# A third set of input buffers for the recurrence, and every third low half of the mixer's weights made by GpSimd

## The reference

```python
def first_block(x, c, norm_g, w_ada, b_ada, w_in, ...):
    mod = silu(c) @ w_ada + b_ada                 # shift, scale, gate
    h = rms(x, norm_g) * (1 + scale) + shift
    proj = h @ w_in                               # 2048 -> 8 * 1024 columns
    a_q, a_k, a_v, a_z, g_q, g_f, g_i, g_z = split(proj)
    att = chunk_attention(a_q, a_k, a_v) * silu(a_z)      # 8 heads of 128
    hg = hgrn2(g_q, g_f, g_i) * silu(g_z)                 # 8 heads of 128
    return x + gate * (concat(att, hg) @ w_out)

def hgrn2(q_raw, f_raw, i, lb, o_g):
    q = silu(q_raw)
    logf = log(lb + (1 - lb) * sigmoid(f_raw))
    k = (1 - lb) * sigmoid(-f_raw)
    # in chunks of 64 rows, with state S and b = cumsum(logf) in the chunk:
    #   o = (q * exp(b)) @ S + sum over s <= t of (q_t . exp(b_t - b_s) . k_s) v_s
    #   S = exp(b_last) * S + (k * exp(b_last - b))^T @ v
    return rms(o, o_g)
```

## Time and profile before

| | before |
|---|---|
| median of 3 runs, us | 1598.51 |
| lowest and highest run, us | 1595.97, 1599.43 |
| span of the profiled execution, us | 1599.0 (the page gives no other time of it) |
| TensorE busy, us | 1573.0 (98%) |
| VectorE busy, us | 1154.1 (72%) |
| ScalarE busy, us | 862.4 (54%) |
| GpSimd busy, us | 151.6 (9%) |
| TensorE's granted clock, mean | 0.994 |

### The profile page before, as it was taken

One profiled execution on the slowest core, in us unless ns is written; L12 is line 12 of the kernel. 1 busy time (PEld: TensorE's weight loads), 2 busy tenths in 40 slices (PEclk: granted clock), 3 DMA queues, 4 the chain that ended last, 5 costly groups with the idle time before them and its releaser, 6 DMA issues.

```text
span 1599.0 us, 24289 instructions
## 1 busy us (share of the span) xinstructions
PE 1573.0 (98%) x9650; PEld 1400.7 (88%) x9650; DVE 1154.1 (72%) x1696; ACT 862.4 (54%) x1321; POOL 151.6 (9%) x164
## 2 busy tenths in 40 slices
PE   8998999989999999999999999999999999999999
PEld 6787889988999999988799888888888888888887
DVE  6797867877778886759778777777777777455544
ACT  6855546767665555655556454544444444444442
POOL 0000000321221220034213000000000000000000
PEclk9999999999999999999999999999999999999999
DMA  9999975533457774343244545555455454555552
GB/s 373 369 343 349 365 285 209 188 114 121 180 189 267 285 272 179 132 158 132 97 144 178 189 170 199 184 186 210 172 197 191 179 211 175 205 199 185 198 196 105
DMA packets 47825, 331.02 MB, mean 207 GB/s; under 512 B 5281, under 2 KB 6689, under 8 KB 8417
## 3 DMA queue, kind: packets, MB, share of 16 engines
q1 hardware_dynamic: 45184, 312.20, 53.5%
q0 software_dynamic: 2240, 17.04, 2.8%
q10 hardware_dynamic: 290, 0.25, 0.1%
HBM read 327.37 MB, written 2.10 MB: 206 GB/s over the span
## 4 chain that ended last, share of the span: by engine, by line
PE 89%; DVE 5%; DMA 3%; ACT 2%; issue 1%; POOL 0%; SPq 0%; ACTq 0%; DVEq 0%; POOLq 0%
PE ps L1173 20%; PE ps L1174 11%; PE ps L1169 9%; PE ps L1170 8%; PE ps L1171 8%; PE ps L1228 5%; PE ps L1227 5%; PE ps L1226 5%; PE ps L1216 4%; PE ps L1217 3%; PE ps L1218 3%; DVE wl L1916 2%; DMA raw<-in_wts 1%; DMA xs<-in_xN 1%; PE ps L1384 1%; PE ps L1351 1%
## 5 line engine op out<-in xcount | busy, mean ns | idle before, releaser
L1916 DVE TENSOR_TENSOR wl<-raw,wh 128x1024 fp32r<-128x1024 f32 x512 | 626.2, 1236 | 282.4 <-ACT wh L1519 281.9
L1519 ACT ACTIVATE wh<-raw 128x1024 fp32r<-128x1024 f32 x512 | 531.3, 1054 | 377.2 <-PE ps L1228 130.6
L1173 PE MATMUL ps<-hA,wh 128*128 128x512 f32 x1408 | 488.7, 390 | 0.0
L1174 PE MATMUL ps<-hA,wl 128*128 128x256 f32 x1408 | 397.0, 282 | 0.0
L1173 PEld LDWEIGHTS ps<-hA,wh 128*128 128x128 f32 x1408 | 264.2, 188 | 55.3
L1174 PEld LDWEIGHTS ps<-hA,wl 128*128 128x128 f32 x1408 | 266.1, 189 | 0.0
L1169 PE MATMUL ps<-hA,wh 128*128 128x256 f32 x752 | 219.5, 292 | 0.0
L1170 PE MATMUL ps<-hA,wh 128*128 128x256 f32 x752 | 211.7, 282 | 0.0
L1171 PE MATMUL ps<-hA,wl 128*128 128x256 f32 x752 | 211.7, 282 | 0.0
L1169 PE MATMUL ps<-hB,wh 128*128 128x256 f32 x576 | 164.4, 285 | 0.8 <-DVE work L2362 0.4
L1170 PE MATMUL ps<-hB,wh 128*128 128x256 f32 x576 | 161.1, 280 | 0.0
(11 more groups left out here) (303 smaller groups left out, 2077.9 us busy)
## 6 DMA issues: line engine op xcount, KB each, us to landing
raw<-in_wts SPq DMA_DIRECT2D x256, 1024.0 KB, 4.8
raw<-in_ada SPq DMA_DIRECT2D x36, 1024.0 KB, 6.1
side<-in_ada POOLq DMA_DIRECT2D x12, 1024.0 KB, 8.5
work<-in_memN SPq DMA_DIRECT2D x2, 1024.0 KB, 8.9
xs<-in_xN POOLq DMA_DIRECT2D x1, 2048.0 KB, 20.6
xs<-in_xT POOLq DMA_DIRECT2D x2, 1024.0 KB, 7.8
out_rows<-xs SPq DMA_DIRECT2D x8, 256.0 KB, 2.4
wp<-in_dt SPq DMA_DIRECT2D x8, 128.0 KB, 2.7
```

The lines of the kernel that those rows point to most:

```text
L1173: e.matmul(ps[bank][:, :], w1, hl, start=first, stop=False)
L1174: i = e.matmul(ps[bank][:, T:2 * T], w2, hl[:, 0:T], start=False, stop=last)
L1519: e.activation(wh[:, h % WS, :], raw[:, n % RAW, part * HALF:(part + 1) * HALF], ACT.Copy).then_inc(s_hi)
L1916: e.tensor_tensor(wl[:, h % WS, :], src, wh[:, h % WS, :].bitcast(F32), ALU.subtract).then_inc(s_lo)
```

## The change

- `fin`, `qin` and `zin` become lists of four: pair 0 and pair 3 share one slot, pair 1 has the other, and pair 2 has a new buffer `third` of three tiles of 128 x 512 (`INPUT_SET = (1, 0, 2, 1)`). It lies in memory that is free in this part of the program.
- The evacuation of pair 2's inputs waits for no other pair, that of pair 3's for pair 0's last step. In the order only the tiles of pair 3 call `until`, for `("rt", 0)`. Since `kks` and `Es` still have two slots, the task `rf` of pairs 2 and 3 now waits by itself for `rt` of the pair two before (`rec_head`).
- While `share` is on, from the mixer's first tile to the end of the first six tiles of `w_out`, every half whose number divides by `POOL_SHARE = 3` has its low half made by GpSimd: halves 84, 87, ... 156, 25 of them. They count on a semaphore of their own, `wlo_pool`. All who waited for a low half (TensorE, and SyncE's queue for a free slot of `raw`) now wait for the counter of the engine that makes it, by `low_done`. The planner books them on GpSimd's clock with 2.6 us instead of on VectorE's with 1.24.

All other steps are the same, in another order: `HOLD` and the costs are unchanged, but the planned clocks run differently. Both orders are equal up to half 84 or so and again from the end of `w_out` on.

```diff
@@
+INPUT_SET = (1, 0, 2, 1)
...
-BLOCK, HI, LO, TTR = 0.35, 1.05, 1.24, 2.4
+BLOCK, HI, LO, POOL_LO, TTR = 0.35, 1.05, 1.24, 2.6, 2.4
+POOL_SHARE = 3
...
                 at = self.run("act", HI, self.pe_at.get(self.split - WS, 0.0))
-                self.low_at[self.split] = self.run("dve", LO, at + HOP) + HOP
+                if self.share and self.split % POOL_SHARE == 0:
+                    self.pool_low.add(self.split)
+                    self.low_at[self.split] = self.run("pool", POOL_LO, at + HOP) + HOP
+                else:
+                    self.low_at[self.split] = self.run("dve", LO, at + HOP) + HOP
...
+    def rec_head(p):
+        while p >= 2 and ("rt", p - 2) not in o.done:
+            yield
+        yield from stages(("rf", p), REC_HEAD)
...
+    o.share = True
     for kind, n in MIX:
-        if kind != "az" and n >= 2:
-            o.until(("rt", n - 2))
+        if kind != "az" and n == 3:
+            o.until(("rt", 0))
...
         if kind == "f":
-            o.add(5, ("rf", n), stages(("rf", n), REC_HEAD))
+            o.add(5, ("rf", n), rec_head(n))
...
         o.s_half(line[i:i + 8], "C")
+    o.share = False
...
+        third = nc.alloc_sbuf_tensor_at("third", [P, 3, 512], F32, offset=hB_off + 32 + 12 * 2048)
...
+        fin, zin, qin = ([(pair[:, 0, :], pair[:, 1, :], third[:, i, :])[n] for n in INPUT_SET] for i, pair in enumerate((fin2, zin2, qin2)))
...
+        def low_done(h):
+            by_pool = sum(n <= h for n in o.pool_low)
+            return (s_plo, by_pool) if h in o.pool_low else (s_lo, h + 1 - by_pool)
...
                 if j == 0:
-                    e.wait_ge(s_lo, h + 1)
+                    e.wait_ge(*low_done(h))
...
                 if k == "sigmoid":
                     e.wait_ge(*after(("f", 2 * pr + 1), "act", "ev"))
+                    if pr >= 2:
+                        e.wait_ge(*after(("rt", pr - 2), "dve", "lo"))
...
                     pr = j // 2
-                    if pr >= 2:
-                        e.wait_ge(*after(("rt", pr - 2), "dve", "lo"))
+                    if pr == 3:
+                        e.wait_ge(*after(("rt", 0), "dve", "lo"))
...
                 if b[0] == "low":
-                    split(*b[1:])
+                    if b[1] not in o.pool_low:
+                        split(*b[1:])
...
+            def split(h, n, part):
+                src = raw[:, n % RAW, part * HALF:(part + 1) * HALF]
+                e.wait_ge(s_hi, h + 1)
+                e.tensor_tensor(wl[:, h % WS, :], src, wh[:, h % WS, :].bitcast(F32), ALU.subtract).then_inc(s_plo)
```

More of the change, by code:

```diff
@@ L253, in __init__ @@
         self.second = set()
+        self.share = False
+        self.pool_low = set()
         self.events = []
@@ L913, in program @@
         s_side = [sem(f"side{i}") for i in range(4)]
-        s_hi, s_lo, s_half, s_mid = (sem(n) for n in ("whi", "wlo", "half", "mid"))
+        s_hi, s_lo, s_plo, s_half, s_mid = (sem(n) for n in ("whi", "wlo", "wlo_pool", "half", "mid"))
         chains = {f"{c}_{e}": sem(f"{c}_{e}") for c in ("ev", "pre", "lane0", "lane1", "lane2", "lane3", "lane4", "lane5")
@@ L965, in program @@
         a1 = 0
-        fin, a1 = carve(a1, 2, 512, of=early)
-        qin, a1 = carve(a1, 2, 512, of=early)
-        zin, a1 = carve(a1, 2, 512, of=early)
+        fin2, a1 = carve(a1, 2, 512, of=early)
+        qin2, a1 = carve(a1, 2, 512, of=early)
+        zin2, a1 = carve(a1, 2, 512, of=early)
+        fin, zin, qin = ([(pair[:, 0, :], pair[:, 1, :], third[:, i, :])[n] for n in INPUT_SET] for i, pair in enumerate((fin2, zin2, qin2)))
         kk, a1 = carve(a1, 512, of=early)
@@ L1121, in load @@
                     else:
-                        e.wait_ge(s_lo, 2 * o.widx[b] + 2)
+                        e.wait_ge(*low_done(2 * o.widx[b]))
+                        e.wait_ge(*low_done(2 * o.widx[b] + 1))
                 src = ada[o.at[n]] if o.entries[n][0] == "a" else wts[o.at[n]]
@@ L1374, in rec_end @@
                     e.wait_ge(*after(t, "act", "sq"))
-                    e.matmul(ps[6][:, :], ones[:], fin[:, t[1] % 2, :], start=True, stop=True).then_inc(mark(t, "pe", "ss"))
+                    e.matmul(ps[6][:, :], ones[:], fin[t[1]], start=True, stop=True).then_inc(mark(t, "pe", "ss"))
             def softmax(t, k, bank, pairs, causal, v, B):
@@ L2091, in rec_end @@
                 pr = t[1]
-                f, r, z = (x[:, pr % 2, :] for x in (fin, qin, zin))
+                f, r, z = (x[pr] for x in (fin, qin, zin))
                 if k == "r1":
@@ L2408, in rec @@
                 pr = t[1]
-                f = fin[:, pr % 2, :]
+                f = fin[pr]
                 def decay(n):
@@ L2498, in ev @@
                     e.wait_ge(*after(t, "pool", "d"))
+            def split(h, n, part):
+                src = raw[:, n % RAW, part * HALF:(part + 1) * HALF]
+                e.wait_ge(s_hi, h + 1)
+                e.tensor_tensor(wl[:, h % WS, :], src, wh[:, h % WS, :].bitcast(F32), ALU.subtract).then_inc(s_plo)
             e.wait_ge(raw_in[2], 16)
             for b in o.beats:
-                if b[0] == "sload":
+                if b[0] == "low":
+                    if b[1] in o.pool_low:
+                        split(*b[1:])
+                elif b[0] == "sload":
                     i = b[1]
```

26 lines of the change are left out of this document (13 added, 13 removed).

## The result

The changed kernel took 1611.69 us (median of 4 runs, 1610.03 to 1615.05), the kernel before 1598.97 (4 runs). The ratio is 1.0088, with a 95% interval of 1.0066 to 1.0111: 12.7 us slower by the medians, 14 by the ratio. The forecast was 1588.5 us with a range up to 1597.0, and 0.07 on slower.

What follows compares the result with a forecast made beforehand. The prediction took the kernel to be bound by TensorE's matmuls, busy 1573.0 of 1599.0 us. It summed 1599.0 - 13.7 + 3.7 + 0 = 1589.0 us, 1588.5 against the median, with a range of 1583.0 to 1597.0.

Steps and rivals of the forecast that it cites:

- The third buffer's gain: Forced waits ahead of pairs 2 and 3 go: 8.5 us idle, 4.2 clock, 1.0 unpacked matmuls, 13.7 us won.
- small matmuls that aren't packed: In the forced stretches, small matmuls' waits below the trace's grain count as busy; 1 us of gain, 0 to 4.
- What is late next: Moved steps crowd ahead of the output projection and at pair 0's and 1's ends: 3.7 us lost, 1 to 8.
- six forced rows: Ahead of the output projection at half 144, TensorE has six rows without a projection block: 1.9 us lost.
- the two old stretches: Forced places behind halves 103 and 111, without projection matmuls: 12.7 us lost on 40 rows, 0.32 us a row.
- Rival 1: Stalls move to pair 3's end at half 152: some 4 us there, 2 scattered, 1594.5 us; chance 0.17.
- GpSimd's low halves: 25 subtractions moved from VectorE to GpSimd, estimated at 1.9 us each; 0 us on the path setting the end.
- the bound of 1.6: At each GpSimd low half, VectorE would lose 1.6 us when its next instruction reads two SBUF inputs.
- my net of -5 us: VectorE's net work from the 25 moved low halves, taken as -5 us, between -31 and +9.
- TensorE never idle at 36 of 40 us: In window 520 to 560 VectorE was busy 35.75 of 40 us, TensorE never idle: VectorE near nine tenths costs nothing.
- Rival 3: VectorE falls behind through port blocking at halves 92 to 108 and 140 to 144: 3 us, 1591.5; chance 0.15.
- rival 2: GpSimd's low halves come late behind decay steps, 1 us TensorE stall at each of 15: 1603.5 us; chance 0.08.

Runs made afterwards that it cites:

- e3_same_order_dve: The changed kernel's order to the row, but VectorE makes the 25 low halves instead of GpSimd: 1603.68 us, ratio 1.0034 to the kernel before.
- e13_no_hold_rec2: As e12_no_hold_rt3, also without the hold table's entries for pair 2's recurrence: 1587.82 us, ratio 0.9933 to the kernel before.
- e6_gates_later: As e3_same_order_dve, with the output gate's sums in the w_out stretch two tiles later: 1594.69 us, ratio 0.9969 to the kernel before.
- e9: The kernel before with only the output gate's sums two tiles later: 1599.81 us, ratio 1.0011 to the kernel before.
- e7_both: As e6_gates_later, with forced waits for attention 4 to 7 and the gates two halves into w_out: 1596.83 us, ratio 0.998.
- e12_no_hold_rt3: As e6_gates_later, without the hold table's two entries for pair 3's end: 1593.66 us, ratio 0.9967 to the kernel before.
- e8: The kernel before's order to the row, two input buffers, but GpSimd makes the 25 low halves: 1603.32 us, ratio 1.0024.
- e10: The changed kernel with only the output gate's sums two tiles later: 1605.62 us, ratio 1.0041 to the kernel before.
- e11: The changed kernel's order to the row, with 37 low halves by GpSimd instead of 25: 1621.45 us, ratio 1.0145.
- e2_pool_only: The changed kernel with two input buffers and the old forced waits, keeping GpSimd's low halves, planner's own order: 1608.01 us, ratio 1.0051.

## Why the prediction was wrong

**The third buffer's gain (13.7 us): the size was right, in another order.** In e3_same_order_dve no idle time and no lower clock is left in halves 80 to 112, where before had 7.6 us idle (no matmul under way) and lost 5.1 us of clock, 4.8 of it while TensorE was busy (the prediction's 8.49 us of idle time has 0.87 in it that lies behind half 112). With the order mended, e13_no_hold_rec2 has 13.2 us less in halves 80 to 156: 11.0 us of idle time and clock, and 2.1 us of what is left besides them, where the prediction had 1 us for small matmuls that aren't packed.

**"What is late next" (3.7 us, 1 to 8): the first step that failed.** Summed over the trace of e3_same_order_dve, idle time and missing clock (the missing share of the clock times its time) are 5.7 + 4.6 us in halves 140 to 144, 4.0 + 1.7 in 152 to 156, 2.0 and 0.8 in 112 to 120 and 136 to 140, and 0.5 of clock between: 19.3 us. I priced six forced rows by the mean loss per row of the two old stretches. But what a forced row costs is what its chain waits for: these stand behind three gate sums of 2.28 us in VectorE's queue, and behind a low half whose weights the sums' raw slots may have kept out. e6_gates_later (-0.65%) against its control e9 (no change) shows that moving this batch matters in this order only; e7_both and e13_no_hold_rec2 show that the forced steps make the rest of it (25.4 and 21.8 down to 13.3 and 14.9 us). The rows of before had these three sums in the same place of the program; I didn't look at what the order puts on VectorE there.

**Rival 1 was right in its place and price (4 us at half 152), and I gave it 0.17.** The wait is 3.97 us, at the row that the prediction named. The cause that it named first, GpSimd's decays behind its low halves, is not it: with all low halves on VectorE (e3_same_order_dve) the wait is 4.0 us as well. The hold table, its argument "for", is a part of it. Its chance should have been near one: the order showed pair 3's result in place 0.4 halves ahead of its use, and the hold table kept `rstd` back by 4.39 us for an order in which that was free. e12_no_hold_rt3 shows it for the 1.5 us that were left when the gate sums' move had taken 2.5; that it alone would take all 4 wasn't run.

**GpSimd's low halves (0 us): the second step that failed.** The size was estimated at 1.9 us; where VectorE leaves it alone a low half took 2.37 to 2.40 us, and 2.77 in the mean. In the four pairs of runs with the same order VectorE lost 1.52 to 1.56 us at each (e8, e10, e11, changed), near the bound of 1.6, and not the smaller loss behind my net of -5 us: its busy time rose by 7.4 us. In e2_pool_only, with an order of its own, it was 1.3. The larger error was to read "TensorE never idle at 36 of 40 us" as "more load costs nothing". As I read it, load taken away where VectorE waits for ScalarE frees nothing, and what VectorE is held up in front of a step of a chain is passed on to TensorE if that chain is waited for; the 1.7 us ahead of half 144 is one place where the rows show it. Same order, e3 against changed: 8.6 us; e6 against e10: 11.5; in the slack order of before, 3.8. Rival 3 named this and priced it at 3 us. That VectorE's blocking is what costs everywhere, and not the later decays in GpSimd's own queue, is not shown: both come with each low half, and no run parts them. The direct part, a wait for GpSimd's `wl`, was 1.3 us, so rival 2 in its own form (1 us at each of 15) is out at 25 low halves and begins at 37 (7.3 us).

**The sum.** 1599.0 - 12.7 (idle and clock of the old stretches) + 19.3 - 0.9 (idle that 112 to 120 had already) + 10.3 gives 1615; the span was 1608.2, 6.8 less. Of these, 3.5 us is an earlier start of half 80 (248.5 against 252.0 us), in a part where both programs are the same, and so luck of the one execution: the granted clock was at its lower level there for 10.2 us before and for 3.4 in the changed kernel, which is 3.4 us of the difference. Of the other 3.3, 1.1 us is idle time at the lower clock that this sum counts twice, and 2.1 us is that halves 80 to 156 take 275.4 us besides idle time and clock in e3_same_order_dve and 277.5 before. By the stretches alone the change costs 12.7 us, as the medians have it.

The rule of the Trainium skill that I cited (page "SBUF — State Buffer", section "SBUF: two separate sides": an exclusive lock for the whole instruction) agrees with this trace: GpSimd's low half at 490.39 begins during a gate sum that runs until 492.57 and ends 2.20 us behind it, somewhat less than the 2.39 it takes alone, and VectorE's low half of 492.74 ends 1.09 us behind GpSimd's, where it takes 1.22 alone. Each waited out the other. It spoke against this change, and I let it change the term of VectorE but not the sum.

## What to carry to other kernels

Taking out a forced wait moves its steps; price what they then stand behind, in every queue that they enter (here a batch of three long sums on VectorE and perhaps the ring slots that these hold), not by what they cost where they stood. A table of delays tuned for one order must be looked through for entries whose slack is gone: the entries of two tasks and one shifted batch turned +0.3% into -0.7%, with VectorE making all low halves. GpSimd was no relief for VectorE on these subtractions of two SBUF inputs: with 1.2 us saved and 1.5 us lost for each, VectorE was the busier for it.

## What I had not expected of the hardware

A subtraction of 128x1024 on GpSimd with nothing beside it took 2.37 to 2.40 us, where 128x512 took 1.04 and 128x256 0.61: more than twice the half size. The output of the larger one is the rounded matmul format, and whether that is the reason wasn't tried. And one GpSimd low half that met a gate sum on VectorE took 4.38 us, 2.0 more than alone; the sum had 2.2 us to run when it began.
